# Second part of the modulation: product and fold over the eight tiles on GpSimd, sum over the partitions on TensorE

## What is computed

```
c_act = silu(c)
mod = c_act @ w_ada + b_ada
sh1, sc1, gt1, sh2, sc2, gt2 = split(mod, 6)
h = rms_norm(x, g_pre_mix) * (1 + sc1) + sh1
proj = h @ w_in                      # q, k, v of group A; latents and index of group B
out_a = sliding_window_sink_attention(...)   # 8 heads, window 128
out_b = dsa_sparse_attention(...)            # 8 heads, 256 best keys of each query
x = x + gt1 * rms_norm(concat(out_a, out_b) @ w_o, g_post_mix)
h2 = rms_norm(x, g_pre_ffn) * (1 + sc2) + sh2
gate, up = split(h2 @ w_gate_up, 2)
x = x + gt2 * rms_norm((silu(gate) * up) @ w_down, g_post_ffn)
```

## Time and profile before

| what | us |
| --- | --- |
| median of three runs | 3482.56 |
| lowest and highest | 3476.46, 3484.5 |
| the profiled execution | 3481.7 |
| its span in the trace | 3479.7 |
| `mixing`, about | 42 to 1750 |

### The profile page before, as it was taken

One profiled execution on the slowest core, in us unless ns is written; L12 is line 12 of the kernel. 1 busy time (PEld: TensorE's weight loads), 2 busy tenths in 40 slices (PEclk: granted clock), 3 DMA queues, 4 the chain that ended last, 5 costly groups with the idle time before them and its releaser, 6 DMA issues. The chain is left out here.

```text
span 3479.7 us, 43432 instructions
## 1 busy us (share of the span) xinstructions
PE 3031.9 (87%) x14889; PEld 2461.0 (71%) x14889; DVE 2096.1 (60%) x3969; ACT 1288.9 (37%) x2575; POOL 120.0 (3%) x245
## 2 busy tenths in 40 slices
PE   5788888878787877876889699999999999999997
PEld 2476666667666666665868588788878788788876
DVE  2168888999999999999445344325432444244422
ACT  1464454555444444443533222223222322222222
POOL 0000000000000000000011000000000000000000
PEclk8787888888887887887999899999999999999999
DMA  5011100000000000000056433234333433343323
GB/s 203 22 46 37 36 29 20 21 19 25 22 19 10 25 22 4 10 4 7 4 188 185 144 96 96 91 122 139 96 93 119 141 96 96 112 145 96 96 87 107
DMA packets 316078, 254.90 MB, mean 73 GB/s; under 512 B 9153, under 2 KB 271905, under 8 KB 315809
## 3 DMA queue, kind: packets, MB, share of 16 engines
q1 hardware_dynamic: 282544, 236.29, 21.8%
q10 hardware_dynamic: 33392, 16.81, 1.7%
HBM read 219.50 MB, written 33.57 MB: 73 GB/s over the span
## 5 line engine op out<-in xcount | busy, mean ns | idle before, releaser
L1119 DVE TENSOR_SCALAR_CACHE_REDUCE above<-score,cand 128x384 bf16<-128x384 f32 (+13 forms) x448 | 662.0, 1478 | 10.3
L1863 DVE TENSOR_TENSOR p_lo<-raw,p_hi 128x1024 fp32r<-128x1024 f32 x264 | 323.5, 1225 | 425.2 <-ACT p_hi L1789 425.0
L1789 ACT ACTIVATE p_hi<-raw 128x1024 fp32r<-128x1024 f32 x264 | 279.4, 1059 | 692.7 <-PE dbank L1760 353.8
L978 ACT ACTIVATE probT<-tbank 128x512 f32<-128x512 f32 (+3 forms) x448 | 216.9, 489 | 491.4 <-PE tbank L707 488.0
L723 PE MATMUL obank<-vb,probT 128*128 128x64 f32 x2176 | 313.3, 289 | 13.5 <-ACT probT L978 13.0
L723 PEld LDWEIGHTS obank<-vb,probT 128*128 128x128 f32 x2176 | 304.2, 213 | 19.2 <-ACT probT L978 18.7
L692 PE MATMUL lbank<-kb,qb_hi 128*128 128x512 f32 (+3 forms) x320 | 168.7, 527 | 163.4 <-DVE mx L1177 129.0
L590 PE MATMUL work<-w_in,h_T 128*128 128x512 f32 (+1 forms) x768 | 303.2, 545 | 0.7 <-ACT h_T L787 0.7
L1741 PE MATMUL gbank<-x_hi,p_hi 128*128 128x512 f32 x704 | 276.2, 392 | 29.5 <-DVE p_lo L1863 29.5
L1758 PE MATMUL dbank<-p_hi,a_hi 128*128 128x512 f32 x704 | 278.2, 395 | 17.0 <-DVE a_lo L1891 14.0
L1759 PE MATMUL dbank<-p_lo,a_hi 128*128 128x512 f32 x704 | 276.8, 393 | 0.0
(11 more groups left out here) (199 smaller groups left out, 5074.7 us busy)
## 6 DMA issues: line engine op xcount, KB each, us to landing
raw<-in_w_gate_up SPq DMA_DIRECT2D x176, 512.0 KB, 3.8
raw<-in_w_down SPq DMA_DIRECT2D x88, 512.0 KB, 3.7
ada<-in_w_ada ACTq DMA_DIRECT2D x32, 512.0 KB, 3.8
wada<-in_w_ada SPq DMA_DIRECT2D x4, 2048.0 KB, 15.5
x_in<-in_x SPq DMA_DIRECT2D x16, 512.0 KB, 3.8
mixT<-oT SPq DMA_DIRECT2D x32, 256.0 KB, 2.3
mix<-mixT SPq DMA_DIRECT2D x16, 512.0 KB, 6.3
x_rows<-in_x SPq DMA_DIRECT2D x16, 512.0 KB, 4.5
```

The costliest lines, as they stand in the source:

```text
L1119: link(nc.vector.tensor_scalar(above[:, 0:L], score[:, 0:L], cand[:].bitcast(F32), None, ALU.is_ge, ALU.add, accum_out=count[:]), between, 1)
L1789: nc.scalar.activation(p_hi[:, s], raw[:, s], ACT.Copy).then_inc(panel_high, 1)
L1863: nc.vector.tensor_tensor(p_lo[:, s], raw[:, s], p_hi[:, s].bitcast(F32), ALU.subtract).then_inc(panel_ready, 1)
```

## The change

The eight tiles of `ada` are no longer multiplied by PE. POOL multiplies `ada` in place with `c_act` (spread over the 128 columns), and folds the eight tiles to four, two and one by three adds in place. PE then multiplies the one tile with a column of ones.

```diff
+        ones_col = sb("ones_col", [P, 1])
...
+        ada_folded = sem("ada_folded")
...
             link(nc.gpsimd.memset(neg_half[:], -0.5))
+            link(nc.gpsimd.memset(ones_col[:], 1.0))
+
+            def fold_ada(n):
+
+                pool.wait_ge(ada_in, 16 * (n + 1))
+                link(nc.gpsimd.tensor_tensor(ada[:], ada[:], shared.c_act[:].unsqueeze(2).to_broadcast([P, KD, P]),
+                                             ALU.mult))
+                link(nc.gpsimd.tensor_tensor(ada[:, 0:4, :], ada[:, 0:4, :], ada[:, 4:8, :], ALU.add))
+                link(nc.gpsimd.tensor_tensor(ada[:, 0:2, :], ada[:, 0:2, :], ada[:, 2:4, :], ALU.add))
+                nc.gpsimd.tensor_tensor(ada[:, 0, :], ada[:, 0, :], ada[:, 1, :], ALU.add).then_inc(ada_folded, 1)
...
             pool.wait_ge(weights_in, 16 * N_W)
+            fold_ada(0)
+            folded, heads_since, seen = 1, 0, set()
             for s in plan.steps:
+                if s[0] == "mod":
+                    heads_since = 0
+                if s[0] == "head":
+                    heads_since += 1
+                    if heads_since == 2 and folded < MOD_STEPS and ("mod", folded - 1) in seen:
+                        fold_ada(folded)
+                        folded += 1
+                seen.add(s)
...
-                pe.wait_ge(ada_in, 16 * (n + 1))
-                for k in range(KD):
-                    mm = nc.tensor.matmul(ps[:, 0:1], ada[:, k, :], shared.c_act[:, k:k + 1],
-                                          start=(k == 0), stop=(k == KD - 1))
-                mm.then_inc(work_full, 1)
+                pe.wait_ge(ada_folded, n + 1)
+                nc.tensor.matmul(ps[:, 0:1], ada[:, 0, :], ones_col[:], start=True, stop=True).then_inc(work_full, 1)
```

## The result

| what | before | changed | ratio |
| --- | --- | --- | --- |
| median of four runs, us | 3481.64 | 3522.23 | 1.0112 (95%: 1.0100 to 1.0124) |
| lowest and highest, us | 3476.46, 3484.5 | 3519.9, 3523.72 | |
| span of the profiled execution, us | 3479.7 | 3521.8 | |

The change costs 40.6 us. The forecast was slower by 21 to 22 us, at 3503.7 us. By the median the measured time lies 0.2 us above the upper end of its range (3522). The ratio is reckoned over all executions and is not the quotient of the two medians (1.0112 x 3481.64 is 39.0 us more). Two later executions of other kernels, 6% longer than the rest of their kernel, are left out of all that follows.

A forecast was written before the change was run, and what follows sets the result against it. PE was taken to bound the first rounds and DVE's search the long rest. 3481.7 us + 29 (DVE stalls left after waits) - 12 (PE's saving) + 5 (start) = 3503.7 us, range 3483 to 3522.

The forecast's parts named there:

- POOL's reads hold DVE: In `mixing`, POOL's folds hold DVE instructions with two SBUF inputs: 43 us, 26 of them in the search.
- (a): In the search, L1126's one-element read slips between POOL's and isn't held: 3484 us, chance 0.15.
- (b): Faster: L1126 not held, start free, folds of steps 9 and 12 in time, PE's saving remains: 3472 us, chance 0.09.
- (d): POOL shuts out every DVE instruction that reads SBUF, counts too: 120 us, 3590 us, chance 0.02.
- Rival (c): POOL's product is slower than L554, or folds hit DVE in each cycle: twice the stall, 3533 us, chance 0.05.
- The start: Fold 0 ahead of the first block's root makes L1048 begin at about 59 instead of 54.25: +5 us, bounds 0 and 6.
- PE's part: Mod steps save PE 1.54 us each; only ten DVE waits for PE count: 14.3 us, 12 after overlap.
- What the waits swallow: About 14 of DVE's 43 us of stalls fall ahead of waits for PE that absorb them, leaving 29.
- + 29 - 12: In the sum for `mixing`: 29 us of DVE stalls left after waits, less 12 us of PE's saving.

The follow-up runs named there:

- e2_pool_alone: Kernel before, plus POOL's four fold instructions on a spare buffer nobody uses; PE's passes unchanged, nothing new waited for: 3502.74 us.
- e3_pool_writes: Kernel before, plus five write-only POOL iotas of 1024 columns on a spare buffer in each fold's place: 3488.41 us.
- e4_fold0_later: Changed kernel with fold 0 behind the first block's root and add in POOL's list instead of ahead of them: 3518.49 us.
- e1_pe_alone: Kernel before, but each mod step multiplies only the first of eight tiles; POOL does nothing new: 3466.64 us.
- e10_a1_whole: Kernel before with POOL folding a spare buffer; mod steps take one tile without waiting for POOL, but the 14 behind head A1 take all eight: 3511.67 us.
- e5_after_8: Changed kernel, still waiting for the fold, but PE multiplies all eight tiles with the ones instead of one: 3518.81 us.

## Why the prediction was right in its sign and short in its size

**POOL's reads hold DVE: right, and in size.** The forecast had 43 us, 26 of them in `cand`. Measured are 43.7 us, some 3 of them at the start, so 40.6 against 43, with 25.8 in `cand`. The forecast's note that `score` beside POOL's add took 2.71 to 2.73 us in all 13 cases holds for twelve; one took 2.58, which changes nothing. Rivals (a), (b) and (d) fall with the 1.814 us, with `e2_pool_alone`, and with the counts (L1138 now), 662.0 us in both pages. The Trainium skill (SBUF — State Buffer, Who interferes with whom) says that a VectorE instruction with two SBUF inputs contends with a GpSimd instruction that reads SBUF, not with one that only writes it, and that the contention is an exclusive lock; the trace agrees down to an instruction of one element per partition, 1.814 us where 0.159 is its median, and agrees again where POOL only writes (`e3_pool_writes`): 0.222 us. Rival (c) has no support in the product, which took 2.00 us where 2.34 was taken, though the time came out between the forecast and its 3533 us. With the shorter product the longest `cand` is 1.81 and not 2.3 us.

**The start: right, but for a small slip.** Forecast +5 us and L1048's successor at 59; measured 58.97, of which 4.0 to 4.7 us is the fold's doing, and 3.7 us in the time of `e4_fold0_later`. The forecast's own terms give a little more than it wrote: 49.3 + 4.8 + 4.9 is 59.0 without the root's 0.9 us, 59.9 with it.

**PE's part: right by itself, for a reason that was half wrong.** `e1_pe_alone` gave 14.5 us, the sum of ten waits was 14.3. But the trace has 30.7 us of shorter waits and 18.3 us of new ones, and 5.7 us of what the profiled execution gained arose behind 1700 us. That the two figures meet so closely is luck. In the first mod steps it is as described: the wait of 2.37 us in the earlier trace rows is now

```profile
155.52 0.48 DVE L1196 CUSTOM_DVE_ANT_0 logit<-lbank,bias_a,neg_sink 128x256 f32<-128x256 f32 x1 [0.77 <-PE lbank L712]
```

**What the waits swallow: right by itself.** The forecast had 14 us. `e2_pool_alone` shows 29.0 shorter and 13.7 new, net 15.3.

**The step that failed is the sum of these two**, "+ 29 - 12". It took 14 us of stalls as swallowed and 12 us of PE's saving as gained, 26 us in all, from the same stock of waits, and set new waits at nothing. Measured in the changed kernel: 22.8 us shorter, and 25.9 us new (0.8 of them at the start). So the term is 25.1 - 22.8 = +2 us and not -26, and with it the whole is 40.6 + 4 + 2 = 47 us in DVE's order, 45.3 by the offset at 1700 us and 42.1 at the end. Were the halves independent, waits would have shrunk by 30.7 + 29.0 - 18.3 - 13.7 = 27.7 us; they grew by 3.1. That is 31 of the 33 us, and the rest is 7 us more of stalls (43.7 against 36.4), less what came back after `mixing`.

Where these 31 us lie can be read by laying the four traces beside each other wait by wait. Three parts come out, 30 us together.

- Some 12 us are waits counted twice. The wait of 2.38 us at 801.24 is gone in `e1_pe_alone`, gone in `e2_pool_alone` and gone in the changed kernel, and so is one of 1.49 us (1489 us). A wait can be filled from either side, by an earlier PE or by a later DVE, but once: the two savings together are 12 us more than the waits were long. The forecast did take off some of this, 2.3 us at two places where a stall and a saving were neighbours; but the shift runs on, so every wait downstream is such a place.
- Some 11 us more stand directly behind the second groups that are slow in the changed kernel. The wait of 4.06 us is 2.12 us in either half, where the second group ahead of it took 3.60 us. In the changed kernel that group took 5.04 us and the wait is back:

```profile
230.76 0.48 DVE L1196 CUSTOM_DVE_ANT_0 logit<-lbank,bias_a,neg_sink 128x256 f32<-128x256 f32 x1 [3.80 <-PE lbank L712]
```

- Some 6 us lie at other places and have no cause here. One wait of 3.79 us (288 us) is 1.58 or 1.59 us long in all three, though neither half had used it up; one of 3.50 us (559 us) is 0.18 in `e2_pool_alone` and 3.41 in the changed kernel.

The 11 us agree with `e10_a1_whole`, which took the second groups that alone are slow from nine to one and the time down by 10.6 us. They show where the cost lies, and not yet why the clock falls there.

**What is settled and what is not.** Settled: POOL's reads cost 21.6 us alone, and the size of the stall follows the length and number of POOL's reading instructions. Settled too: PE's missing passes turn from a gain of 14.5 us into a loss of 20 once those reads are there, and PE's waits for POOL aren't needed for it. That waits were counted twice is shown at single waits, for 12 of the 31 us. Why 25.9 us of new waits arose is only partly shown: seven of them, 11.2 us, stand behind second groups at a lower clock; eleven second groups are slow in the changed kernel and six of them already in `e1_pe_alone` (new waits of 1.0, 1.7, 1.4 and 1.5 us). But filling PE's idle time did not bring them back. And `e5_after_8` leaves open what the dependence alone does: where the passes stay, it costs 16 us by the medians with only four second groups slow alone.

**The range.** Its upper end came from half as much stall again. The stall hardly was off at all; the term for the waits was, by 28 us, and it had no bounds of its own. That the measured time came so near to the range's end is luck. Had the range let the waits give nothing, its upper end would have been 3481.7 + 43 + 5 = 3530 us.

## What to carry to other kernels

A saving on one engine and a stall on the other are both paid from the waits between the two, so when a change brings both, count the stock of waits once, allow for new ones, and take as the other bound that it gives nothing. Beside a VectorE chain with two inputs in SBUF, GpSimd work that reads SBUF costs up to the rest of each of its instructions: cutting a fold of four into fifteen instructions made GpSimd 70 us busier and the kernel 27 us faster. A matmul engine that is merely less busy gains nothing behind a point where it waits anyway. In this kernel the stretch at the lower clock then moved to a group that VectorE waited for.

## What the runs showed of the hardware that was not expected

- POOL's product whose second input is one value spread over 128 columns took 1.90 us for 1024 columns at its shortest, 2.00 on average. The add of two full inputs of that size takes 2.34 us at the least.
- POOL instructions that only write hold DVE's copies (0.29 to 1.12 us for 128 x 256), and twice its one-input `score<-relu,widx` of 128 x 512 (0.48 to 0.97 and 1.03 us), but not `cand` or `score`, which have two inputs in SBUF and began beside an iota 57 and 14 times.
- POOL and DVE lengthen each other at the start: the product took 3.53 us and the cast beside it 2.80 us, where 1.90 us is the product's shortest and 1.23 us the cast's length in the trace of before. In the search, against that, the product mostly kept its length (2.00 us on average), and DVE's instruction was the one that was held.
- PE's mean clock between 100 and 1700 us fell from 0.82 to 0.80 with less work on PE. The total of its idle time in `mixing` (42 to 1750 us before, 43 to 1796 in the changed kernel) rose from 350 to 429 us.
